# Attention outputs made as features by tokens, row sums taken by the product, top-k rounds spread

## The chip, the cores and the metric

The kernel runs on one core of one Trainium2 chip. Its engines are TensorE (PE, with PEld for the loading of its stationary operand), VectorE (DVE), ScalarE (ACT), GpSimd (POOL) and SyncE (SP), which here only issues DMAs. The metric is the device time of one execution in microseconds (us); the median of the runs shown is compared.

## The reference

One streaming step of a hybrid encoder layer on 512 prompt tokens and 64 tokens of a running stream with 128 cached keys (D = 1024, float32). In the part that the change touches, eight query heads with two key/value heads of 64 features attend to keys that an indexer has chosen:

```python
index_score = jnp.einsum('bqh,bqhl->bql', w_idx * IDX_SCALE, jax.nn.relu(dots))
index_score = jnp.where(admissible[None], index_score, -jnp.inf)
_, sel = lax.top_k(index_score, topk)                  # topk = min(256, keys / 4)
...
logits = jnp.einsum('bqgrd,bqkgd->bqgrk', qg, k_sel) * (hd ** -0.5)
p = jax.nn.softmax(jnp.where(valid, logits, -jnp.inf), axis=-1)
o = jnp.einsum('bqgrk,bqkgd->bqgrd', p, v_sel)         # then o @ w_branch_dsa
```

Around it stand an RMSNorm, one input projection (`x @ w_in`), a gated linear recurrence, a merge with gates, and a convolutional feed-forward part. The outputs are the layer's tokens and the new keys, values and states.

## The kernel before

The order of all work in the first part is written out as a list of slots (`plan_slots`). A slot is one weight block of the projection applied to all tokens, or, for the value weights of the recurrence (`gv`), one weight panel applied to one of five token tiles (tile 0: the 64 sample tokens, tiles 1 to 4: 128 prompt tokens each). The four gv panels have five such slots each, with a short slot `z` for the gate logits after the second. Each engine runs through the same list; beside the slot's own work it does what `plan_aux` has put at that slot. Nothing reorders this at run time: every engine works its instructions in order and waits on semaphores.

Attention is put in as 40 steps `("att", n)`, one a slot, 8 heads for each tile in the order 1, 0, 2, 3, 4. Step n is a pipeline over four heads: PE makes the logits of head n (L2260, L2261) and DVE adds the mask and takes the minimum of the negated values (L1666); ACT exponentiates, with the row sum as accumulator (L1127); PE turns the probabilities of head n-2 (L2269) and ACT copies them to SBUF (L1122, for the sample tile L1119); PE multiplies the turned probabilities of head n-3 with the values (L2283), and DVE divides the 64 columns of the head by the row sum (L1673, L1678) into `otok`, tokens by features. After each eighth head PE turns `otok` into features by tokens (L2291), and ACT copies that to `aqt` (L1137), in which the queries of the same tile stood. Since the turn uses a logits bank, PE waits at steps 12, 20, 28 and 36 for that copy (`o_ready`). Every fourth step also splits four heads of queries for the next tile into a rounded part (ACT L1055, `q_split`) and its remainder (DVE L1593).

The mask of tiles 0, 2, 3, 4 comes from top-k on DVE: a round takes the 8 largest scores (MAX8, L1651) and strikes them out (L1652). Tile 0 has 6 rounds of 192 keys, the others 16 rounds each of 256, 384 and 512 keys. `plan_aux` gives out rounds by a budget: each slot from the first attention step on adds `ATT_ROOM` to it, and a round of w keys takes 2w + 220 from it:

```python
while n < len(rounds) and AT_IDX + rounds[n][0] < s and room > 0:
    put(s, ("topk", rounds[n:n + 1]))
    room -= 2 * width(IDX_TILES[rounds[n][0]]) + 220
    n += 1
```

DVE also does a scan for each `z` slot, one slot later (L1686, L1687, L1689, after a softplus on ACT, L1142 to L1144), and three multiplications two slots after that (L1694 to L1698). The split of a weight panel into rounded part and remainder is ACT's (L960) and, for the panels of this stretch, POOL's (L789); from the `gr` panels on DVE does it (L1531). POOL also stores the new keys and values to HBM before its first split. All products are sums of three (rounded times rounded, and the two cross terms with the remainders), except those in attention and recurrence in plain float32.

Of the kernel before, what the change touches and what calls it, by code (L numbers as in the profile page):

```python
# [178 lines left out]
ATT_ROOM = 1800  # L179
# [121 lines left out]
def layer_kernel(nc, A, O):  # L301
# [6 lines left out]
    with ExitStack() as ctx:  # L308
# [49 lines left out]
        v_low = at("v_low", [P, TILES, 148], F32, o1 + 15872 + 5120)  # L358
        cache = at("cache", [P, 3, P], F32, o1 + 23968)
# [19 lines left out]
        otok = at("otok", [P, QH * HD], F32, o3 + 16128)  # L379
# [70 lines left out]
        probs_turned, pt_ready, pv_done, o_scaled = sem("probs_turned"), sem("pt_ready"), sem("pv_done"), sem("o_scaled")  # L450
        o_turned, o_ready = sem("o_turned"), sem("o_ready")
# [152 lines left out]
        def _(sp):  # L604
# [17 lines left out]
            def saved_load(k):  # L622
                b, j = SAVED_BUFFER[k], SAVED[k]
                if k == 0:
                    sp.wait_ge(o_ready, len(ATT_TILES))
# [20 lines left out]
            for p in range(UP0 + SEVEN0):  # L646
                load(p)
                for what, k in SAVED_MOVES.get(p, ()):
                    if what == "in":
                        saved_load(k)  # L650
                    else:
                        saved_store(k)
                if p == 0:
                    for tt in range(2, TILES):
                        load_x(tt)
                if p == 1:
                    ck, cv = A["cache_k"][0, 0], A["cache_v"][0, 0]
                    sp.dma_start(cache[:, 0, :], ck.rearrange("s g d -> s (g d)")).then_inc(cache_loaded, 16)
                    sp.dma_start(cache[:, 1, :], cv.rearrange("s g d -> s (g d)")).then_inc(cache_loaded, 16)
                    for half in range(2):  # L660
                        sp.dma_start(cache[:, 2, half * 64:half * 64 + 64], A["cache_k_idx"][0, 0]).then_inc(cache_loaded, 16)
                    sp.wait_ge(xlo_ready, 2 * TILES)
                    sp.dma_start(wgu_in[0:RANK, :], A["w_gla_gate_up"][0]).then_inc(wgu_loaded, 16)
# [73 lines left out]
        def _(pool):  # L737
# [29 lines left out]
            pool.wait_ge(coefs_turned, 1)  # L767
            link(nc.gpsimd.memset(bias0[:, :], 0.0))
# [11 lines left out]
            pool.dma_start(O["v_s"][0, 0].rearrange("s g d -> s (g d)"), v_low[0:DEC, 0, 20:148]).then_inc(stored, 16)  # L780

# [11 lines left out]
            for s, slot in enumerate(SLOTS):  # L793
# [7 lines left out]
                for op, n in AUX.get(s, []):  # L801
# [17 lines left out]
                    if op == "gla":  # L819
                        step, tt = GLA_STEPS[n]  # L820
                        if n == 0:
                            pool.wait_ge(o_ready, len(ATT_TILES))
# [121 lines left out]
        def _(act):  # L944
# [61 lines left out]
            for tt in range(TILES):  # L1006
                act.wait_ge(kv_done, tt + 1)
                nc.scalar.activation(k_idx[:, tt, 0:192], ps[:, tt, 0:192], ACT.Copy)
                nc.scalar.activation(k_idx[:, tt, 192:256], ps[:, tt, 128:192], ACT.Copy)
                nc.scalar.activation(v_low[:, tt, :], ps[:, tt, 192:340], ACT.Copy).then_inc(kv_copied, 1)  # L1010
# [46 lines left out]
            def aux(op, n):  # L1057
# [53 lines left out]
                elif op == "att":  # L1111
# [19 lines left out]
                    m = n - 4  # L1131
                    if m >= 0 and m % QH == QH - 1:
                        t = m // QH
                        tt = ATT_TILES[t]
                        act.wait_ge(o_turned, t + 1)
                        k = rows(tt)
                        nc.scalar.activation(aqt[:, :, tok(tt).start:tok(tt).start + k],  # L1137
                                             ps[:, 4 + (n + 1) % 2, :].rearrange("p (b c) -> p b c", b=4)[:, :, 0:k], ACT.Copy).then_inc(o_ready, 1)
# [376 lines left out]
        def _(dve):  # L1515
# [80 lines left out]
            def aux(op, n):  # L1596
# [58 lines left out]
                elif op == "att":  # L1655
# [14 lines left out]
                    if 0 <= m < NATT:  # L1670
                        h = m % QH
# [5 lines left out]
                        g = h // (QH // KVH)  # L1677
                        nc.vector.tensor_scalar(otok[:, HD * h:HD * h + HD], ps[:, 7, HD * g:HD * g + HD],  # L1678
                                                rinv[:, m % 2:m % 2 + 1], None, ALU.mult).then_inc(o_scaled, 1)
# [387 lines left out]
        def _(pe):  # L2067
# [141 lines left out]
            def aux(op, n):  # L2209
# [6 lines left out]
                elif op == "keyt":  # L2216
# [10 lines left out]
                    pe.transpose(ps[:, 7, 0:128], cache[:, 0, :], ident[:, :])  # L2227
                    pe.transpose(ps[:, 7, 128:192], k_idx[0:DEC, 0, 0:128], i64)
                    pe.transpose(ps[:, 7, 192:320], cache[:, 2, :], ident[:, :])
# [15 lines left out]
                elif op == "att":  # L2245
                    if n < NATT:
# [11 lines left out]
                        if n >= 12 and (n - 5) % QH == QH - 1:  # L2258
                            pe.wait_ge(o_ready, (n - 5) // QH + 1)
# [12 lines left out]
                    if 0 <= m < NATT:  # L2272
                        tt = ATT_TILES[m // QH]
                        pe.wait_ge(pt_ready, m + 1)
                        if m >= 1:
                            pe.wait_ge(o_scaled, m)
                        blocks = key_blocks(tt)
                        for i, (c, k) in enumerate(blocks):
                            if tt == 0:
                                val = cache[:, 1, :] if i == 0 else v_low[0:DEC, 0, 20:148]  # L2280
                            else:
                                val = v_low[:, i + 1, 20:148]
# [3 lines left out]
                    m = n - 4  # L2286
                    if m >= 0 and m % QH == QH - 1:

                        pe.wait_ge(o_scaled, m + 1)
                        for b in range(4):  # L2290
                            ins = pe.transpose(ps[:, 4 + (n + 1) % 2, P * b:P * b + P], otok[:, P * b:P * b + P], ident[:, :])  # L2291
                        ins.then_inc(o_turned, 1)
                elif op == "gla":
                    step, tt = GLA_STEPS[n]
                    stream = 0 if tt == 0 else 1
                    if step == "a":
                        if n == 0:
                            pe.wait_ge(sample_values, 5)
                            pe.wait_ge(decay_used, 3 * GH)
                            pe.wait_ge(o_ready, len(ATT_TILES))  # L2300
# [251 lines left out]
```

## Time and profile before

| | us |
|---|---|
| median of 3 runs (973.52 to 974.26) | 973.52 |
| the profiled execution | 974.0 |
| its span, first to last instruction | 972.3 |
| PE busy (98% of the span) | 955.3 |
| DVE busy (64%) | 617.5 |
| ACT busy (49%) | 476.3 |
| POOL busy (19%) | 181.0 |

The granted clock of TensorE is 0.999 of full speed over the span, 2.4 GHz. Attention lies between 86.8 us, the first logits, and 271.6 us, the last copy of the outputs. A row of the timeline or of the chain gives the start and the length in us; in square brackets stands how long the engine was idle before it and who released it. Lengths of PE instructions overlap, so that the spacing of starts, not the length, says what one of them costs.

### The profile page before, as it was taken

Reading aid. Unit: us, or ns where it says so; the run is one execution under the profiler, and the core shown is the slowest. Engines: PE = TensorE matmul, PEld = TensorE weight load, DVE = VectorE, ACT = ScalarE, POOL = GpSimd, SP = SyncE. Lnnn points to the kernel's source line nnn. Section 1 sums busy time; section 2 is a strip of 40 time slices with the busy share of each in tenths; the row PEclk is TensorE's granted clock in tenths of the full one; section 3 lists DMA queues with packets and bytes.
Section 4 is the critical chain, followed back from the end, with each engine's and each line's share of the span. In section 5 each row is a group of like instructions: output and inputs, shape, how many; then the busy total and the mean of one; then the engine's idle time right before and its main releaser. Section 6 shows DMA issues by size and latency. Waiting matters only on the chain.

```text
span 972.3 us, 17124 instructions
## 1 busy us (share of the span) xinstructions
PE 955.3 (98%) x6550; PEld 904.3 (93%) x6550; DVE 617.5 (64%) x997; ACT 476.3 (49%) x800; POOL 181.0 (19%) x301
## 2 busy tenths in 40 slices
PE   8999999999999999999999999999999999999997
PEld 6999998889999999999998899999999999788886
DVE  6278878745344368924455679688888889723214
ACT  6356436777322256421124558566666667522112
POOL 3104423323122111101001146211111112100000
PEclk9999999999999999999999999999999999999999
DMA  6812121112376458766446352244443344412323
GB/s 169 205 45 87 44 88 44 44 44 67 122 235 223 139 209 268 262 242 227 125 135 239 129 174 87 76 121 127 150 123 119 119 128 131 145 36 84 137 70 119
DMA packets 121980, 129.75 MB, mean 133 GB/s; under 512 B 14884, under 2 KB 103828, under 8 KB 119619
## 3 DMA queue, kind: packets, MB, share of 16 engines
q1 hardware_dynamic: 115474, 105.97, 35.0%
q0 software_dynamic: 6448, 22.99, 6.7%
q8 instruction: 39, 0.64, 0.3%
q14 instruction: 19, 0.15, 0.0%
HBM read 105.84 MB, written 23.11 MB: 133 GB/s over the span
## 4 chain that ended last, share of the span: by engine, by line
PE 90%; DVE 4%; ACT 3%; issue 2%; DMA 0%; POOL 0%; DVEq 0%; SPq 0%; ACTq 0%; POOLq 0%
PE ps L2078 11%; PE ps L2080 11%; PE ps L2079 11%; PE ps L2443 7%; PE ps L2445 7%; PE ps L2444 7%; PE ps L2087 7%; PE ps L2089 7%; PE ps L2088 7%; PE ps L2283 2%; PE ps L2097 1%; PE ps L2098 1%; PE ps L2420 1%; PE ps L2419 1%; PE ps L2418 1%
## 5 line engine op out<-in xcount | busy, mean ns | idle before, releaser
L2078 PE MATMUL ps<-xs,whi 128*128 128x288 f32 x608 | 183.4, 302 | 0.0
L2080 PE MATMUL ps<-xs,wlo 128*128 128x288 f32 x608 | 179.1, 295 | 0.0
L2079 PE MATMUL ps<-xs,whi 128*128 128x288 f32 x608 | 179.0, 294 | 0.0
L1531 DVE TENSOR_TENSOR wlo<-raw,whi 128x2048 fp32r<-128x2048 f32 (+2 forms) x36 | 78.9, 2193 | 107.9 <-ACT whi L960 107.9
L960 ACT ACTIVATE whi<-raw 128x2048 fp32r<-128x2048 f32 (+2 forms) x47 | 86.1, 1833 | 99.3 <-PE ps L2089 76.4
L2078 PEld LDWEIGHTS ps<-xs,whi 128*128 128x128 f32 x608 | 114.2, 188 | 0.7
L2079 PEld LDWEIGHTS ps<-xs,whi 128*128 128x128 f32 x608 | 114.2, 188 | 0.4
L2080 PEld LDWEIGHTS ps<-xs,wlo 128*128 128x128 f32 x608 | 114.0, 188 | 0.0
L2087 PE MATMUL ps<-whi,xs 128*128 128x256 f32 (+2 forms) x224 | 72.7, 325 | 0.1
L2089 PE MATMUL ps<-wlo,xs 128*128 128x256 f32 (+2 forms) x224 | 71.2, 318 | 0.0
L2088 PE MATMUL ps<-whi,xs 128*128 128x256 f32 (+2 forms) x224 | 71.2, 318 | 0.0
L789 POOL TENSOR_TENSOR wlo<-raw,whi 128x512 fp32r<-128x512 f32 x36 | 45.8, 1303 | 128.6 <-ACT whi L960 128.6
L2089 PE MATMUL ps<-wlo,us 128*128 128x512 f32 x176 | 69.5, 395 | 0.0
L2087 PE MATMUL ps<-whi,us 128*128 128x512 f32 x176 | 69.5, 395 | 0.0
L2088 PE MATMUL ps<-whi,us 128*128 128x512 f32 x176 | 69.5, 395 | 0.0
L2445 PE MATMUL ps<-ts,wlo 128*128 128x288 f32 x216 | 63.9, 296 | 0.0
L2444 PE MATMUL ps<-ts,whi 128*128 128x288 f32 x216 | 63.7, 295 | 0.0
L2443 PE MATMUL ps<-ts,whi 128*128 128x288 f32 x216 | 63.5, 294 | 0.0
L2087 PEld LDWEIGHTS ps<-whi,xs 128*128 128x128 f32 x224 | 42.5, 190 | 3.2 <-DVE xs L1557 0.4
L2089 PEld LDWEIGHTS ps<-wlo,xs 128*128 128x128 f32 x224 | 42.5, 190 | 2.5
L2088 PEld LDWEIGHTS ps<-whi,xs 128*128 128x128 f32 x224 | 42.5, 190 | 2.4
L1040 ACT ACTIVATE stage<-ps 128x576 f32<-128x576 f32 x24 | 15.6, 652 | 57.6 <-PE ps L2080 57.6
(370 smaller groups left out, 2616.8 us busy)
## 6 DMA issues: line engine op xcount, KB each, us to landing
raw<-in_w_in SPq DMA_DIRECT2D x21, 1024.0 KB, 5.8
raw<-in_w_down SPq DMA_DIRECT2D x10, 1024.0 KB, 5.0
saved<-in_w_up SPq DMA_DIRECT2D x36, 256.0 KB, 4.3
sums_scratch<-saved SPq DMA_DIRECT2D x9, 1024.0 KB, 4.8
raw<-sums_scratch SPq DMA_DIRECT2D x9, 1024.0 KB, 4.8
qraw<-in_w_up SPq DMA_DIRECT2D x27, 256.0 KB, 2.9
raw<-in_w_up SPq DMA_DIRECT2D x13, 512.0 KB, 4.0
raw<-in_w_up SPq DMA_DIRECT2D x26, 256.0 KB, 4.5
```

What stands on the lines that cost most here:

```text
L789: ins = nc.gpsimd.tensor_tensor(wlo[:, p % 2, c], raw[:, p % 2, c], whi[:, p % 2, c].bitcast(F32), ALU.subtract)
L960: nc.scalar.activation(whi[:, p % 2, 0:n], raw[:, p % 2, 0:n], ACT.Copy).then_inc(hi_ready, 1)
L1531: nc.vector.tensor_tensor(wlo[:, p % 2, 0:n], raw[:, p % 2, 0:n], whi[:, p % 2, 0:n].bitcast(F32), ALU.subtract).then_inc(lo_ready, 1)
L2078: pe.matmul(out, wh[:, k, c0:c0 + P], xh[:, k, t], start=(k == 0), stop=False)
L2079: pe.matmul(out, wh[:, k, c0:c0 + P], xl[:, k, t], start=False, stop=False)
L2080: ins = pe.matmul(out, wl[:, k, c0:c0 + P], xh[:, k, t], start=False, stop=(k == kn - 1))
L2087: pe.matmul(out, xh[:, k0 + k, t], wh[:, k, :], start=(first and k == 0), stop=False)
L2088: pe.matmul(out, xl[:, k0 + k, tl or t], wh[:, k, :], start=False, stop=False)
L2089: ins = pe.matmul(out, xh[:, k0 + k, t], wl[:, k, :], start=False, stop=(last and k == kn - 1))
L2443: pe.matmul(out, wh[:, c], xh[:, k, :], start=(opens and k == 0), stop=False, skip_group_check=True)
L2444: pe.matmul(out, wh[:, c], xl[:, k, :], start=False, stop=False, skip_group_check=True)
L2445: ins = pe.matmul(out, wl[:, c], xh[:, k, :], start=False, stop=(k == 3), skip_group_check=True)
```

## The change

The values become the stationary operand of the product and the turned probabilities the moving one, so the product comes out as features by tokens and needs no turn. Beside the 64 value features of a head's group stand 64 columns of ones, so the other 64 rows of the same product hold the row sum, once in each row. DVE takes the reciprocal of those 64 rows (64 x 128) and multiplies the 64 rows of features by it, straight into `aqt`. For the ones, `v_low` becomes 64 columns wider, and POOL moves the values of the second group and sets the ones after the stores; the cached values are loaded in two pieces with room for ones between. `otok`, its turn, the copy by ACT, the accumulator of the exponential and the waits on both go; `o_ready` is now given once a head. `ATT_ROOM` falls from 1800 to 1300.

```diff
-ATT_ROOM = 1800
+ATT_ROOM = 1300
...
# SP: load of the cached values
-sp.dma_start(cache[:, 1, :], cv.rearrange("s g d -> s (g d)")).then_inc(cache_loaded, 16)
+sp.dma_start(cache[:, P:P + 4 * HD].rearrange("p (a b) -> p a b", b=HD)[:, 0:3:2, :], cv).then_inc(cache_loaded, 16)
...
# POOL, behind the stores
+pool.wait_ge(stored, 16 * 6)
+link(nc.gpsimd.tensor_copy(v_low[:, :, 20 + 2 * HD:20 + 3 * HD], v_low[:, :, 20 + HD:20 + 2 * HD]))
+nc.gpsimd.memset(v_low[:, :, 20 + HD:20 + 2 * HD], 1.0).then_inc(values_spread, 1)
...
# ACT, step n
 nc.scalar.activation(lg[:, n % 3, 0:w], lg[:, n % 3, 0:w], ACT.Exp, bias=negmax[:, n % 3:n % 3 + 1],
-                     scale=-1.0, accum_out=rowsum[:, n % 4:n % 4 + 1]).then_inc(probs_ready, 1)
+                     scale=-1.0).then_inc(probs_ready, 1)
...
-        act.wait_ge(o_turned, t + 1)
-        nc.scalar.activation(aqt[:, :, tok(tt).start:tok(tt).start + k],
-                             ps[:, 4 + (n + 1) % 2, :].rearrange("p (b c) -> p b c", b=4)[:, :, 0:k], ACT.Copy).then_inc(o_ready, 1)
...
# DVE, step n, head m = n - 3
-dve.wait_ge(probs_ready, m + 1)
-link(nc.vector.reciprocal(rinv[:, m % 2:m % 2 + 1], rowsum[:, m % 4:m % 4 + 1]))
 dve.wait_ge(pv_done, m + 1)
-if m >= QH and h == 0:
-    dve.wait_ge(o_turned, m // QH)
-nc.vector.tensor_scalar(otok[:, HD * h:HD * h + HD], ps[:, 7, HD * g:HD * g + HD],
-                        rinv[:, m % 2:m % 2 + 1], None, ALU.mult).then_inc(o_scaled, 1)
+link(nc.vector.reciprocal(rec[of_v, 0:k], ps[of_sum, 7, 0:k]))
+nc.vector.tensor_tensor(aqt[half, h // 2, tok(tt).start:tok(tt).start + k], ps[of_v, 7, 0:k], rec[of_v, 0:k],
+                        ALU.mult).then_inc(o_ready, 1)
...
# PE, step n
-if n >= 12 and (n - 5) % QH == QH - 1:
-    pe.wait_ge(o_ready, (n - 5) // QH + 1)
...
-if m >= 1:
-    pe.wait_ge(o_scaled, m)
+if m == 0:
+    pe.wait_ge(values_spread, 1)
+    pe.wait_ge(pads_zero, 3)
+else:
+    pe.wait_ge(o_ready, m)
...
-    ins = pe.matmul(ps[:, 7, 0:128], pt[0:k, m % 2, P * i:P * i + P], val,
+    ins = pe.matmul(ps[:, 7, 0:q], val, pt[0:k, m % 2, P * i:P * i + q],
                     start=(i == 0), stop=(i == len(blocks) - 1))
...
-    pe.wait_ge(o_scaled, m + 1)
-    for b in range(4):
-        ins = pe.transpose(ps[:, 4 + (n + 1) % 2, P * b:P * b + P], otok[:, P * b:P * b + P], ident[:, :])
-    ins.then_inc(o_turned, 1)
```

How instructions stand on two engines, first on DVE at attention steps 26 and 27 (third gv panel, tile 3 with 384 keys), before. `lg` are the masked logits, `score_92` the mask of 384 keys in this list, and the two ISA rows are the masking and its minimum:

```order
L1666 ISA lg,small<-ps,score_92 128x384
L1666 ISA small 128x1
L1673 RECIPROCAL small<-small 128x1
L1678 TENSOR_SCALAR otok<-ps,small 128x64
L1666 ISA lg,small<-ps,score_92 128x384
...
L1593 TENSOR_TENSOR q_split<-aqt,q_split 64x512
L1686 SCALAR_TENSOR_TENSOR tmp<-tmp 128x576
```

The same place after the change, where `score_91` is the mask of 384 keys and `score_92` the scores of 512 keys:

```order
L1662 ISA lg,small<-ps,score_91 128x384
L1662 ISA small 128x1
L1672 RECIPROCAL rec<-ps 64x128
L1673 TENSOR_TENSOR aqt<-ps,rec 64x128
L1647 MAX small<-score_92 128x8
L1648 MATCH_REPLACE score_92<-small,score_92 128x512
L1647 MAX small<-score_92 128x8
L1648 MATCH_REPLACE score_92<-small,score_92 128x512
L1662 ISA lg,small<-ps,score_91 128x384
...
L1589 TENSOR_TENSOR q_split<-aqt,q_split 64x512
L1681 SCALAR_TENSOR_TENSOR tmp<-tmp 128x576
```

Between the two maskings stand now two rounds of top-k of 512 keys, which stood some ten steps earlier before, and the reciprocal has grown from one column to 64 x 128.

On PE at step 19 (end of the first gv panel), where the outputs of the sample tile are turned, before:

```order
L2260 MATMUL ps<-k_hi,q_split 128x256
L2261 MATMUL ps<-k_lo,q_split 128x256
L2269 MATMUL ps<-ident,lg 128x128 x2
L2283 MATMUL ps<-v_low,pt 128x128 x2
L2291 MATMUL ps<-ident,otok 128x128 x4
L2097 MATMUL ps<-whi,xs 128x256
```

The same place after the change:

```order
L2253 MATMUL ps<-k_hi,q_split 128x256
L2254 MATMUL ps<-k_lo,q_split 128x256
L2262 MATMUL ps<-ident,lg 128x128 x2
L2280 MATMUL ps<-pt,v_low 128x128 x2
L2092 MATMUL ps<-whi,xs 128x256
```

The four turns of `otok` are gone, the product has as many instructions as before, with its operands exchanged, and PE goes on to the weights of the next panel.

## Rows read from the trace of the kernel before

**Rows 1.** The page: busy time by engine, and the chain's shares.
```profile
PE 955.3 (98%) x6550; PEld 904.3 (93%) x6550; DVE 617.5 (64%) x997; ACT 476.3 (49%) x800; POOL 181.0 (19%) x301
...
PE 90%; DVE 4%; ACT 3%; issue 2%; DMA 0%; POOL 0%; DVEq 0%; SPq 0%; ACTq 0%; POOLq 0%
```

**Rows 2.** Waits of PE, 80 to 290 us: total, times, longest.
```profile
PE ps L2260 <- ACT aqt L1137: 4.1, 2, 2.3
PE ps L2269 <- ACT pt L1122: 1.4, 2, 0.8
PE ps L2283 <- DVE otok L1678: 1.0, 2, 0.6
```

**Rows 3.** Timeline of PE, steps 20 and 28: idle before, releaser.
```profile
165.97 0.35 PE L2260 MATMUL ps<-k_hi,q_split 128*128 128x256 f32 x1 [1.76 <-ACT aqt L1137]
...
202.85 0.41 PE L2260 MATMUL ps<-k_hi,q_split 128*128 128x384 f32 x1 [2.31 <-ACT aqt L1137]
```

**Rows 4.** Windows: stretch, length, busy PE, PEld, DVE, ACT, POOL, clock, DMA.
```profile
143.80:164.20 20.40, 20.40 (x160) 19.12 (x158) 17.95 (x42) 14.96 (x31) 7.42 (x6) 1.00 0.17 53
164.20:186.80 22.60, 19.05 (x156) 18.45 (x155) 19.85 (x49) 15.28 (x30) 7.58 (x6) 1.00 0.15 47
186.80:210.40 23.60, 20.70 (x171) 20.09 (x170) 11.38 (x31) 18.34 (x36) 6.15 (x6) 1.00 0.15 46
210.40:232.60 22.20, 22.20 (x181) 21.66 (x180) 12.29 (x28) 16.84 (x30) 7.43 (x6) 1.00 0.16 48
```

**Rows 5.** The chain near the last attention steps: start, length.
```profile
267.10 0.89 PE ps L2283 x8
...
271.15 0.44 PE ps L2291 x4
```

**Rows 6.** Timeline of PE in the recurrence: 64 moving columns.
```profile
291.38 0.39 PE L2312 MATMUL ps<-qk,k_cross 128*128 128x64 f32 x2
291.60 0.39 PE L2311 MATMUL ps<-qk 128*128 128x64 f32 x2
```

**Rows 7.** Lines of DVE by form: busy us, mean ns, idle before.
```profile
L1722 DVE RECIPROCAL tmp<-tmp 128x576 f32<-128x576 f32 x4 | 15.0, 3754 | 5.6 <-ACT tmp L1177 5.4
...
L1678 DVE TENSOR_SCALAR otok<-ps,small 128x64 f32<-128x64 f32 x40 | 11.4, 284 | 12.0 <-PE ps L2283 8.1 <-PE ps L2291 3.0
...
L1673 DVE RECIPROCAL small<-small 128x1 f32<-128x1 f32 x40 | 6.3, 158 | 0.0
...
L1932 DVE TENSOR_TENSOR hb<-ps,p 128x64 f32<-128x64 f32 x18 | 3.9, 219 | 0.0
...
L2008 DVE TENSOR_TENSOR us<-u_all,us 128x128 fp32r<-128x128 f32 x1 | 0.3, 283 | 0.0
```

**Rows 8.** Timeline of DVE: rounds of top-k that follow each other.
```profile
117.34 0.55 DVE L1651 MAX8 small<-score 128x8 f32<-128x384 f32 x1
...
118.58 0.56 DVE L1651 MAX8 small<-score 128x8 f32<-128x384 f32 x1
...
142.16 0.68 DVE L1651 MAX8 small<-score 128x8 f32<-128x512 f32 x1
...
143.66 0.69 DVE L1651 MAX8 small<-score 128x8 f32<-128x512 f32 x1
```

**Rows 9.** Waits of DVE, 143.8 to 210.4 us: total, times, longest.
```profile
DVE q_split L1593 <- ACT q_split L1055: 6.7, 4, 4.2
DVE lg L1666 <- PE ps L2261: 6.4, 3, 3.1
DVE tmp L1686 <- ACT tmp L1144: 1.2, 2, 0.9
```

**Rows 10.** Timeline of DVE: the query split of step 27.
```profile
202.26 0.69 DVE L1593 TENSOR_TENSOR q_split<-aqt,q_split 64x512 fp32r<-64x512 f32 x1 [4.16 <-ACT q_split L1055]
```

**Rows 11.** Timeline of POOL: the last store and what follows.
```profile
42.17 0.53 POOL L780 DMA_DIRECT2D out_v_s<-v_low  x1
75.22 5.08 POOL L789 TENSOR_TENSOR wlo<-raw,whi 128x512 fp32r<-128x512 f32 x4 [32.51 <-ACT whi L960]
```

More of the change, by code:

```diff
@@ L378, in layer_kernel @@
         pt = at("pt", [P, 2, 512], F32, o3 + 12032)
-        otok = at("otok", [P, QH * HD], F32, o3 + 16128)
+        cache = at("cache", [P, 3 * P + HD], F32, o3 + 16128)
+        rec = at("rec", [P, P], F32, o3 + 17920)
         gain_row = at("gain_row", [P, D], F32, o3 + 5888)
@@ L657, in _ @@
                     ck, cv = A["cache_k"][0, 0], A["cache_v"][0, 0]
-                    sp.dma_start(cache[:, 0, :], ck.rearrange("s g d -> s (g d)")).then_inc(cache_loaded, 16)
-                    sp.dma_start(cache[:, 1, :], cv.rearrange("s g d -> s (g d)")).then_inc(cache_loaded, 16)
+                    sp.dma_start(cache[:, 0:P], ck.rearrange("s g d -> s (g d)")).then_inc(cache_loaded, 16)
+                    sp.dma_start(cache[:, P:P + 4 * HD].rearrange("p (a b) -> p a b", b=HD)[:, 0:3:2, :], cv).then_inc(cache_loaded, 16)
                     for half in range(2):
-                        sp.dma_start(cache[:, 2, half * 64:half * 64 + 64], A["cache_k_idx"][0, 0]).then_inc(cache_loaded, 16)
+                        sp.dma_start(cache[:, 2 * P + HD + half * 64:3 * P + half * 64], A["cache_k_idx"][0, 0]).then_inc(cache_loaded, 16)
                     sp.wait_ge(xlo_ready, 2 * TILES)
@@ L1009, in _ @@
                 nc.scalar.activation(k_idx[:, tt, 192:256], ps[:, tt, 128:192], ACT.Copy)
-                nc.scalar.activation(v_low[:, tt, :], ps[:, tt, 192:340], ACT.Copy).then_inc(kv_copied, 1)
+                nc.scalar.activation(v_low[:, tt, 0:148], ps[:, tt, 192:340], ACT.Copy).then_inc(kv_copied, 1)
             def copy_unit(slot):
@@ L1670, in aux @@
                     if 0 <= m < NATT:
-                        h = m % QH
-                        dve.wait_ge(probs_ready, m + 1)
-                        link(nc.vector.reciprocal(rinv[:, m % 2:m % 2 + 1], rowsum[:, m % 4:m % 4 + 1]))
+                        tt, h = ATT_TILES[m // QH], m % QH
+                        g = h // (QH // KVH)
+                        k, half = rows(tt), slice(64 * (h % 2), 64 * (h % 2) + 64)
+                        of_v, of_sum = slice(HD * g, HD * g + HD), slice(HD - HD * g, 2 * HD - HD * g)
                         dve.wait_ge(pv_done, m + 1)
-                        if m >= QH and h == 0:
-                            dve.wait_ge(o_turned, m // QH)
-                        g = h // (QH // KVH)
-                        nc.vector.tensor_scalar(otok[:, HD * h:HD * h + HD], ps[:, 7, HD * g:HD * g + HD],
-                                                rinv[:, m % 2:m % 2 + 1], None, ALU.mult).then_inc(o_scaled, 1)
+                        link(nc.vector.reciprocal(rec[of_v, 0:k], ps[of_sum, 7, 0:k]))
+                        nc.vector.tensor_tensor(aqt[half, h // 2, tok(tt).start:tok(tt).start + k], ps[of_v, 7, 0:k], rec[of_v, 0:k],
+                                                ALU.mult).then_inc(o_ready, 1)
                     if n % 4 == 3 and n + 5 < NATT:
@@ L2274, in aux @@
                         pe.wait_ge(pt_ready, m + 1)
-                        if m >= 1:
-                            pe.wait_ge(o_scaled, m)
+                        if m == 0:
[3 more added lines that the diff above has]
+                            pe.wait_ge(o_ready, m)
                         blocks = key_blocks(tt)
+                        q, g = rows(tt), m % QH // (QH // KVH)
                         for i, (c, k) in enumerate(blocks):
                             if tt == 0:
-                                val = cache[:, 1, :] if i == 0 else v_low[0:DEC, 0, 20:148]
+                                val = cache[:, P + HD * g:2 * P + HD * g] if i == 0 else v_low[0:DEC, 0, 20 + HD * g:148 + HD * g]
                             else:
-                                val = v_low[:, i + 1, 20:148]
-                            ins = pe.matmul(ps[:, 7, 0:128], pt[0:k, m % 2, P * i:P * i + P], val,
+                                val = v_low[:, i + 1, 20 + HD * g:148 + HD * g]
+                            ins = pe.matmul(ps[:, 7, 0:q], val, pt[0:k, m % 2, P * i:P * i + q],
                                             start=(i == 0), stop=(i == len(blocks) - 1))
                         ins.then_inc(pv_done, 1)
-                    m = n - 4
-                    if m >= 0 and m % QH == QH - 1:
-                        pe.wait_ge(o_scaled, m + 1)
-                        for b in range(4):
-                            ins = pe.transpose(ps[:, 4 + (n + 1) % 2, P * b:P * b + P], otok[:, P * b:P * b + P], ident[:, :])
-                        ins.then_inc(o_turned, 1)
                 elif op == "gla":
```

23 lines of the change are left out of this document (9 added, 14 removed).

## The prediction

> **What bounds the kernel now.** I read the busy shares and the chain of waits first: TensorE (PE) is busy in 98% of the span and makes up 90% of the chain that ended last [rows 1]. So PE work that goes, or a PE wait that goes, is worth its full length, and work on another engine costs nothing until PE waits for it. Then I read who makes PE wait during the attention stage (80 to 290 us) [rows 2]: 4.1 us for the ScalarE (ACT) copy of the turned outputs, 1.4 us for the ACT copy of the turned probabilities, 1.0 us for the scaling on VectorE (DVE), 6.5 us in all. The two waits of the first kind, 1.76 and 2.31 us, are single places [rows 3]. Last I cut the stretch in which they lie into the four panels of value weights (gv 0 to 3, attention steps 15-19, 20-24, 25-29, 30-34) and read the busy time of each engine in each [rows 4]. PE works 20.40, 19.05, 20.70 and 22.20 us in stretches of 20.4, 22.6, 23.6 and 22.2 us, so all 6.45 us of idle time lie in panels two and three. DVE is busy 17.95, 19.85, 11.38 and 12.29 us: nearly as long as PE in the first two panels, with half its time free in the last two. DVE is the engine behind the stalls, and it is also where the change puts its work.
>
> **The change part by part.**
>
> *Turns that go.* Five times PE turns four blocks of the outputs. In the chain one such group of four takes 0.44 us [rows 5]. 5 x 0.44 = 2.2 us of pure PE time go. The ACT copies and the accumulator reads that go are no gain by themselves: ACT waits for others in this stage.
>
> *The product of probabilities and values.* Stationary and moving operand change places; blocks and passes stay. A product of four blocks takes 0.89 us before [rows 5], and for 128 queries all sizes are the same. For the sample tile the moving side shrinks from 128 to 64 columns in 16 products. The nearest row is in the recurrence stage: a two-pass product with 64 moving columns starts 0.22 us after the one before it [rows 6], and a block of the attention product with 128 columns takes 0.89 / 4 = 0.22 us. I take no gain; the far bound, half of 16 x 0.22 us, is 1.8 us.
>
> *Row sums in the product, division by a tensor.* This is the dear part. Before, each of 40 head products costs DVE a reciprocal of one column, 0.158 us, and a scaling of 64 columns, 0.284 us [rows 7], together 0.44. After, it is a reciprocal of 64 x 128 and a tensor_tensor of 64 x 128 (64 x 64 for the 8 sample products). No such reciprocal is in the trace; the bounds are the one of 576 elements, 3.754 us, and the one of 1 element, 0.158 us [rows 7]. The slope is (3.754 - 0.158) / 575 = 6.25 ns an element, so 128 elements cost 0.158 + 127 x 0.00625 = 0.95 us and 64 cost 0.55 us. The multiplication lies at 0.28 us (128 elements) and 0.22 us (64 elements) [rows 7]. New pair: 1.23 and 0.77 us, that is +0.79 and +0.33 us a product; over all, 32 x 0.79 + 8 x 0.33 = 27.9 us more on DVE. If the reciprocal went at the pace of the tensor_tensor of 128 elements, 0.283 us, the pair would cost 0.57 and the surplus be 0.13 us: that end is kept for a rival. I take the slope, because it comes from the same operation.
>
> The Trainium skill (page "VectorE: DVE Perf Modes", section on the TRN2 errata) gives VectorE one price for every operation that reads PSUM, 120 cycles plus one an element at 0.96 GHz, about 0.26 us here. By that the pair would cost 0.54 us, the surplus be 0.10 us, and the sum come out as in the cheap rival below. The same page says that Reciprocal is an iterative divide with a repeat count, and the trace sides with that: 3.754 us for 576 elements.
>
> *Top-k spread.* ATT_ROOM falls from 1800 to 1300, so the rounds of the largest tile (512 keys, 16 rounds), which stood in panels one and two, move later. From the order of the instructions, rounds of 512 in panels one to four: before 7, 4, 0, 0 (five more earlier), after 4, 5, 5, 2, and two rounds of 384 slip into panel one. A round is MAX8 and MATCH_REPLACE8; two rounds start 1.50 us apart at 512 and 1.24 us at 384 [rows 8].
>
> *DVE by panel.* (The one closing operation of a tile moves with its rounds and is left out.) Panel one: rounds -3 x 1.50 + 2 x 1.24 = -2.0; products 4 x 0.33 + 0.79 = +2.1; sum +0.1. Panel two: one round more, +1.5; five products, +3.95; sum +5.45. Panel three: five rounds, +7.5, and +3.95; sum +11.45. Panel four: two rounds, +3.0, and +3.95; sum +6.95. DVE's work becomes 18.1, 25.3, 22.8 and 19.2 us beside 20.4, 19.05, 20.7 and 22.2 us of PE work. In panels two and three it is DVE that has more to do.
>
> *What PE then waits for.* Over the first three panels DVE has 49.2 + 17.0 = 66.2 us. On top come its waits for ACT in the same stretch, 6.7 us for the query split and 1.2 us for the gate chain [rows 9]; these are in program order and not filled by other work. The longest, 4.2 us before the split of step 27, ends at 202.26 us [rows 10]: two rounds (3.0) and two dearer products (1.6) now fall into the time from step 26 to that split, but ACT's chain starts only when DVE has done step 26, so I let it shrink by 1.1 us only. 66.2 + 6.8 = 73.0 us. PE has 60.15 us less two groups of turns, 59.3. The surplus is 13.7 us. DVE may end the third panel farther behind PE than it began the first, but a product is waited for one step later, and a step is 4 us (20.4 / 5): with some lag at the start already, I allow 3 us. So PE idles 10.7 to 13.7 us; I take 12.0. Panel four, 19.2 us and the gate chain's wait against 22.2, about breaks even, and outside the four panels DVE has room: 12.0 is all.
>
> *The two waits that go* are inside this account: without the wait for the turned copy at step 20 PE meets, right behind it, the scaling of step 16; without the one at step 28 it meets the exponential of step 26 and, a step later, the product behind the DVE scan. What was late next before is later still now.
>
> *Edits at no cost.* POOL now waits for its six stores before it spreads the values, with its weight splits queued behind. The last store is issued at 42.2 us, and the next POOL work starts at 75.2 us after 32.5 us of idle [rows 11]. If that cover were gone, the price would be two POOL operations of 128 x 320, under the 1.3 us that each of a weight split's four operations of 128 x 512 takes (5.08 / 4), so under 2.6 us. The strided load of the cached values, twice as many pieces of half the size, is issued on SP's queue at the program's start and read first in the attention stage. That PE needs the spread values at step 3 costs nothing by the same gap on POOL.
>
> **Sum**, against the profiled execution (974.0 us, span 972.3): -2.2 (turns) + 12.0 - 6.45 (idle after less idle before) = +3.35, 977.35 us. The median of the runs shown, 973.52, is 0.5 us under that execution, so I predict 976.9 us. What this kernel's measurement can tell from no change is about 0.2%, 1.9 us: faster is below 971.6, slower above 975.5.
>
> **Rivals.**
> *A: DVE's free time absorbs it.* Within the first three panels DVE waited 6.4 us for logits of PE [rows 9], free time, and the spread evens out the peaks that stall PE now. Then idle time only grows to about 8 us: 974.0 - 2.2 + 1.5 - 0.5 = 972.9 us, no difference. Against it: the free time lies in panel three, and the rounds moved there (7.5 us) fill it before the dearer products come.
> *B: the reciprocal is cheap, and the kernel faster.* At 0.283 us the products add 4 x 0.1 + 11 x 0.13 = 1.8 us in three panels instead of 10.0, the surplus falls from 13.7 to 5.5, less 0 to 3 carried, so 4.0 us of idle: 974.0 - 2.2 - 2.4 - 0.5 = 968.9 us. It decides from a pair of about 0.6 us. Only the row of 576 elements speaks against it, but it is the same operation. The rule of the skill's page above would end here.
> *C: DVE never catches up.* Nothing is carried (13.7), and two further peaks of the size of the first stall now (1.76) come in panel four and behind it, where the gate scan and the weight splits share DVE with the dearer products: idle 17.2 us, 974.0 - 2.2 + 10.8 - 0.5 = 982.1 us. For it: the last round of top-k now ends one step before its scores are used.
>
> **How the numbers follow.** Forecast 0.50 (975 to 979.5), A 0.20, B 0.13, C 0.17. Faster is B, 0.13. Within 0.2% is A and the lower edge of the forecast, 0.25. Slower is the rest, 0.62. The range reaches down to A with most of the sample products' gain and up to C: 971.5 to 982.0, which leaves out B and the end of C.
>
> **What would show it.** The reciprocal in the profile after: 0.9 to 1.0 us for 64 x 128 proves the price, under 0.4 proves B. PE's idle time between steps 15 and 30 should be 10 to 14 us, released by DVE's multiplication into the features or by ACT's exponential, which itself waits for DVE; no turn and no copy behind it is left. DVE should be busy in over nine tenths of panels two and three. I am wrong if PE idles less than 8 us there, or if it waits on something outside the attention stage.

## The result and the profile after

The changed kernel takes 980.53 us (median of 4 runs, 979.72 to 981.05), the kernel before 973.72 us: ratio 1.0067, interval [1.0055, 1.0079], slower by 6.8 us. Slower was forecast, by 3.4 us; 980.5 lies inside the range. The profiled execution took 980.58 us with a span of 978.8 us, 6.5 us over the span before.

The page of the changed kernel, busy time and the chain's shares, beside [rows 1]:
```profile
PE 956.4 (98%) x6530; PEld 905.3 (92%) x6530; DVE 651.5 (67%) x997; ACT 469.5 (48%) x755; POOL 181.2 (19%) x304
...
PE 86%; DVE 7%; ACT 3%; issue 3%; DMA 0%; POOL 0%; DVEq 0%; SPq 0%; ACTq 0%; POOLq 0%
```
PE's share of the chain fell by 4 points and DVE's rose by 3: more of the path now runs through DVE. Who makes PE wait, 80 to 300 us of the changed kernel (total, times, longest), beside [rows 2]:
```profile
PE ps L2280 <- DVE aqt L1673: 10.5, 8, 3.2
PE ps L2262 <- ACT pt L1126: 1.3, 2, 0.7
PE ps L2262 <- ACT pt L1124: 0.2, 1, 0.2
```
The waits for the turned copy are gone, as they must be. In their place the product of a step waits eight times, 10.5 us in all, for the multiplication that empties its bank; the three lines together are 12.0 us, where the three before were 6.5. What that multiplication stands behind is in the lines of DVE by form (busy us, mean ns, idle before), beside [rows 7]:
```profile
L1672 DVE RECIPROCAL rec<-ps 64x128 f32<-64x128 f32 x32 | 30.6, 955 | 5.6 <-PE ps L2280 4.7
...
L1673 DVE TENSOR_TENSOR aqt<-ps,rec 64x128 f32<-64x128 f32 x32 | 9.2, 289 | 1.1
...
L1672 DVE RECIPROCAL rec<-ps 64x64 f32<-64x64 f32 x8 | 4.4, 555 | 1.5 <-PE ps L2280 1.4
...
L1673 DVE TENSOR_TENSOR aqt<-ps,rec 64x64 f32<-64x64 f32 x8 | 1.8, 222 | 0.3
```
The reciprocal has the price that its slope gave: 0.955 and 0.555 us against 0.95 and 0.55. The four gv panels of the changed kernel (steps 15, 20, 25, 30 and 35 begin at 142.9, 163.6, 187.3, 215.6 and 239.9 us), columns as in [rows 4]:
```profile
142.90:163.60 20.70, 19.63 (x156) 18.71 (x155) 17.86 (x40) 14.79 (x29) 7.08 (x6) 1.00 0.17 53
163.60:187.30 23.70, 20.59 (x157) 19.93 (x156) 22.41 (x42) 15.06 (x26) 7.43 (x6) 0.93 0.15 45
187.30:215.60 28.30, 22.30 (x167) 21.25 (x166) 24.15 (x49) 16.31 (x26) 6.15 (x6) 0.94 0.12 38
215.60:239.90 24.30, 22.43 (x180) 21.49 (x179) 22.79 (x38) 16.60 (x25) 7.59 (x6) 1.00 0.15 45
```
Length less PE's busy time is PE's idle time: 1.1, 3.1, 6.0 and 1.9 us, together 12.05. And there is something that the profiled execution of the kernel before does not show in this stage: in panels two and three the granted clock is 0.93 and 0.94. Cut into microseconds around the longest stall of panel two and that of panel three:
```profile
170.00:171.00 1.00, 0.49 (x3) 0.52 (x4) 0.93 (x3) 0.35 (x2) 0.00 (x0) 0.88 0.00 0
171.00:172.00 1.00, 1.00 (x7) 1.00 (x6) 0.93 (x4) 0.00 (x0) 0.00 (x0) 0.50 0.00 0
...
174.00:175.00 1.00, 1.00 (x10) 1.00 (x10) 0.96 (x3) 1.00 (x2) 0.24 (x1) 0.92 0.09 16
...
211.00:212.00 1.00, 0.63 (x4) 0.66 (x5) 0.94 (x3) 0.97 (x4) 0.00 (x0) 0.86 0.00 0
212.00:213.00 1.00, 1.00 (x7) 1.00 (x6) 0.96 (x3) 1.00 (x3) 0.00 (x0) 0.50 0.00 0
```
At 0.50 (1.2 GHz) the clock stays for 3.4 us each time (0.88, three times 0.50, 0.92 in the first); this is called a half-clock stretch below. The timeline of PE shows what went before, and what it costs:
```profile
170.51 0.97 PE L2280 MATMUL ps<-pt,v_low 128*128 128x128 f32 x4 [2.00 <-DVE aqt L1673]
...
171.76 0.41 PE L2082 MATMUL ps<-whi,xs 128*128 128x256 f32 x1
171.97 0.41 PE L2083 MATMUL ps<-whi,xs 128*128 128x256 f32 x1
...
174.26 0.28 PE L2082 MATMUL ps<-whi,xs 128*128 128x256 f32 x1
174.38 0.29 PE L2083 MATMUL ps<-whi,xs 128*128 128x256 f32 x1
...
211.37 1.31 PE L2280 MATMUL ps<-pt,v_low 128*128 128x128 f32 x6 [3.19 <-DVE aqt L1673]
```
PE had stood still for 2.00 and for 3.19 us. Behind that, weight products start 0.21 us apart instead of 0.12, so a stretch of 3.4 us loses 3.4 x (1 - 0.12 / 0.21) = 1.46 us, the two 2.9 us. First account: idle +5.6, half clock +2.9, turns -2.2 = +6.3 of the 6.5 us of span. Whether the clock is a cause or only the form that a wait takes, the account does not say.

### The profile page after: what moved, and what is told of

It reads as the page before. It is cut to its first block, busy times and chain, and to the rows that moved or that the text cites. A ratio compares the mean times of both kernels' runs of the same rounds, so it can differ in the third digit from the quotient of the medians.

```text
span 978.8 us, 17005 instructions
## 1 busy us (share of the span) xinstructions
PE 956.4 (98%) x6530; PEld 905.3 (92%) x6530; DVE 651.5 (67%) x997; ACT 469.5 (48%) x755; POOL 181.2 (19%) x304
## 4 chain that ended last, share of the span: by engine, by line
PE 86%; DVE 7%; ACT 3%; issue 3%; DMA 0%; POOL 0%; DVEq 0%; SPq 0%; ACTq 0%; POOLq 0%
PE ps L2073 11%; PE ps L2075 11%; PE ps L2074 11%; PE ps L2433 7%; PE ps L2435 7%; PE ps L2434 7%; PE ps L2082 6%; PE ps L2084 6%; PE ps L2083 6%; PE ps L2092 1%; PE ps L2093 1%; PE ps L2410 1%; PE ps L2409 1%; PE ps L2408 1%; PE ps L2280 1%
```

## The experiments

The first theory: DVE has too much to do beside the panels; the reciprocal's price is the cost, the spread moves it, the two falls of the clock add 3 us. Rivals: the spread alone costs; each product is delayed by its own longer way through DVE; the clock fell for another reason. A median below stands beside 973.7 to 974.4 us for the kernel before, measured beside it; ratios are to that.

**The price of the division: a copy in its place.**
```
-  reciprocal(rec[of_v, 0:k], ps[of_sum, 7, 0:k])
+  tensor_copy(rec[of_v, 0:k], ps[of_sum, 7, 0:k])
```


> The changed kernel with the reciprocal replaced by a copy of the same 64 x 128 sums (this leaves out the division: the output is multiplied by the sum). Everything else, the product, the spread and the waits, stays. Theory: the copy takes 0.25 to 0.3 us, DVE has 0.67 us less a product, PE's idle time falls to 4 to 6 us, both half-clock stretches go, 969 to 971 us, faster than the kernel before. Rival 1 (the spread is what costs): idle time stays above 9 us, 976 us or more. Rival 3 (the clock fell for another reason than the long stalls): the stretches at half clock are still there, about 3 us on top.

975.41 us, ratio 1.0016 [1.0007, 1.0025]: 5.1 us under the changed kernel, but not the 969 to 971 expected; PE's idle time is 7.75 us (220 less 212.25), not 4 to 6. The copy takes 0.289 us (64 x 128), so 0.67 us a product is worth 5.1 us in all. What stayed, in PE's timeline of this kernel (idle before, releaser):
```profile
169.85 0.68 PE L2280 MATMUL ps<-pt,v_low 128*128 128x128 f32 x4 [1.99 <-DVE aqt L1673]
...
208.72 1.62 PE L2280 MATMUL ps<-pt,v_low 128*128 128x128 f32 x6 [2.54 <-DVE aqt L1673]
```
The two long stalls stand, and a half-clock stretch follows each. The theory misses something that is not the reciprocal's price alone.

**DVE's time without the longer way**: before, with a reciprocal that nobody reads.
```
     tensor_scalar(otok[...], ps[...], rinv[...], None, ALU.mult)
+    reciprocal(spare[0:64, 0:k], ident[0:64, 0:k])
```


> The kernel before with a spare reciprocal (64 x 128, for the sample 64 x 64) on DVE behind each scaling, into a tile that nothing reads: DVE's time for the division without its place in the chain from product to next product, with the old order of the top-k rounds and the old turns. Theory (DVE's sum of work in panels one to three is what delays PE): 0.95 us a product, 5 us in each panel, PE's idle time in the attention stage rises from 6.5 to 11 to 14 us, 978 to 981 us. Rival 2 (it is the longer way from a product to the next one through DVE that PE waits for): 974 to 975.5 us.

979.49 us, ratio 1.0060 [1.0046, 1.0074], +5.7 us: as the theory has it, and the rival, that only the longer way costs, falls. The stalls take another form than expected. PE's waits in this kernel, 80 to 300 us:
```profile
PE ps L2263 <- ACT aqt L1138: 5.3, 3, 2.3
PE ps L2272 <- ACT pt L1123: 2.0, 2, 1.8
PE ps L2286 <- DVE otok L1679: 0.7, 2, 0.5
```
Nearly all of it is put down to ACT, although only DVE got more work: ACT's exponential and copies stand behind DVE's masking, for which ACT waits 40.5 us between 80 and 300 us (19.9 before). PE is idle for 8.65 us there (220 less 211.35 busy), 2.2 more than before, not the expected 5 to 8 more. One half-clock stretch (185 to 189 us) adds 1.5, and 0.5 us lie ahead of the stage (first logits at 87.35 us, 86.84 before); 0.7 us of the 4.9 us of span I can't place.

**No spread.**
```
-ATT_ROOM = 1300
+ATT_ROOM = 1800
```


> The changed kernel with ATT_ROOM back at 1800: dear division, no spread of the top-k rounds. Theory (DVE has too much to do beside the panels: the reciprocal's price is the cost, the spread only moves it, and the clock falls add to it): DVE then has about 20, 24, 15 and 16 us of work in the four panels, so only panel two is over PE's 19 us, and the idle time moves forward and shrinks from 12 to 8 to 11 us; 975 to 979 us, nearer the lower end if no stall reaches 2 us and the clock stays up. Rival 1 (the spread is what costs, the division alone is absorbed): 971 to 973 us. Rival 2 (each product is delayed by its own chain product, reciprocal, multiplication, whatever the order): 980 to 981 us, stalls as many as with the spread.

978.74 us, ratio 1.0059 [1.0045, 1.0073]: inside the theory's 975 to 979, idle 12.6 us (220 less 207.44) rather than 8 to 11, no half-clock stretch in the profiled execution. The division without the spread costs 5.0 us, the turns' gain already taken off. The five runs lie apart: three at 978.28 to 978.74 us with a mean granted clock of 0.999, two at 980.65 and 980.76 with 0.995, the mean that the changed kernel has with its two half-clock stretches. In this kernel the lower clock goes with 2.2 us more.

**The spread alone**, in the kernel before.
```
-ATT_ROOM = 1800
+ATT_ROOM = 1300
```

> The kernel before with ATT_ROOM 1300 instead of 1800: the spread alone, with the cheap scaling. Theory: the rounds move into panels three and four, where DVE had 9 us and 10 us beside PE's work; idle time of PE stays at 6 to 9 us, the clock stays up, 973 to 976 us. Rival 1 (the spread is what costs): idle of 10 us or more, 978 us or more. A third outcome, that the spread by itself evens DVE out as it is said to: idle of 3 to 5 us, 970 to 972 us.

976.83 us, ratio 1.0030 [1.0019, 1.0041]: +3.1 us, over the theory's 976 and under the rival's 978. Idle time is 7.24 us (6.45 before), but it has gathered in one place. DVE's timeline in this kernel, with ACT's exponential of step 26:
```profile
191.67 0.69 DVE L1651 MAX8 small<-score 128x8 f32<-128x512 f32 x1
...
193.78 0.62 ACT L1127 ACTIVATE lg<-lg,small 128x384 f32<-128x384 f32 x1 [0.81 <-DVE small L1666]
...
197.76 0.28 DVE L1678 TENSOR_SCALAR otok<-ps,small 128x64 f32<-128x64 f32 x1
203.30 0.69 DVE L1593 TENSOR_TENSOR q_split<-aqt,q_split 64x512 fp32r<-64x512 f32 x1 [5.26 <-ACT q_split L1055]
```
ACT's same exponential in the kernel before:
```profile
192.74 0.61 ACT L1127 ACTIVATE lg<-lg,small 128x384 f32<-128x384 f32 x1
```
And PE's timeline with the spread, at step 28:
```profile
203.90 0.47 PE L2260 MATMUL ps<-k_hi,q_split 128*128 128x384 f32 x1 [3.48 <-ACT aqt L1137]
```
A round that moved here (191.67 us) stands ahead of the masking of step 26, and ACT's exponential waits for that masking. It starts 1.04 us later than before, and with it all that ACT does next in order: a weight split, the logarithm of the gate chain between two table loads, the high half of the queries and the copy for which PE waits. So PE's stall grows by 1.17 us (3.48 against 2.31), and DVE waits 5.26 us for the high half of the queries, with its next work queued behind. [Rows 10] shows the same wait before, 4.16 us. A half-clock stretch follows the stall of 3.48 us: 0.8 + 1.5 are the 2.3 us of the span.

**The clock**: work for PE in the two long stalls of the changed kernel, ahead of the product's wait.
```
+  if n in (21, 29):
+      pe.wait_ge(masked, n)
+      for _ in range(5 if n == 21 else 6):
+          pe.matmul(ps[:, 4 + (n + 1) % 2, 0:P], ident[:, :], ident[:, :], start=True, stop=True)
```


> The changed kernel with five and six idle products of the identity on PE ahead of the wait for the scaling in steps 21 and 29, behind a wait for the masking of the same step (which DVE ends about 1.3 us earlier than that scaling): the stalls of 2.00 and 3.19 us are cut to about 0.6 and 1.7 us, each followed by work. Theory on the clock (the granted clock fell because PE had stood idle for those 2.00 and 3.19 us): no half-clock stretch behind them, 3.0 us less, 977 to 978.5 us. If one of the two pieces left is still enough for a fall: 979 us. Rival 3 (the fall has another reason): both stretches are still there, 980 to 981.5 us.

979.85 us, ratio 1.0061 [1.0047, 1.0074]: in the profiled execution (980.29 us) the clock stays up, but in the median only 0.7 us come back, not 2 to 3.5. Nor is it the clock that gives these 0.7 us: the three runs with a mean clock of 0.999 took 979.85 to 980.33 us, the two with 0.997 were the quickest (979.53 and 979.57). Windows of this kernel over both places:
```profile
169.00:174.00 5.00, 4.47 (x37) 4.45 (x38) 4.77 (x13) 2.56 (x5) 0.00 (x0) 1.00 0.01 3
208.00:213.00 5.00, 3.11 (x27) 2.90 (x26) 4.83 (x9) 2.72 (x6) 0.00 (x0) 1.00 0.16 58
```
Stalls of 0.69 and 1.89 us, each with work behind it, bring no fall here. So both stretches hang on the two long stalls; that a long stall always brings one does not follow, since the kernel without the spread shows stalls of 2.00 and 2.65 us without. Where the 3 us went is in PE's timeline:
```profile
179.49 0.41 PE L2262 MATMUL ps<-ident,lg 128*128 128x128 f32 x2 [0.91 <-ACT pt L1126]
...
185.15 0.68 PE L2284 MATMUL ps<-pt,v_low 128*128 128x128 f32 x4 [1.36 <-DVE aqt L1673]
...
220.40 0.91 PE L2284 MATMUL ps<-pt,v_low 128*128 128x128 f32 x6 [0.85 <-DVE aqt L1673]
```
The changed kernel has no such wait at the first and third of these places and 0.87 us at the second; later it waits 0.69 us where this one waits 0.97 (230.2 us): 0.91 + 0.49 + 0.85 + 0.28 = 2.5 us of new waits. What PE loses at half clock is, in this kernel, time in which DVE catches up. My theory's third part falls for this kernel: the clock did not add 3 us, it took the place of 2.5 us of waiting.

**The wait in DVE's order**: the low half of the queries' split one attention step later, in the changed kernel and in the kernel before.
```
-  if n % 4 == 3 and n + 5 < NATT:
-      query_lo(n // QH + 1, n % QH // 4)
+  if n % 4 == 0 and 4 <= n < NATT - 4:
+      query_lo((n - 1) // QH + 1, (n - 1) % QH // 4)
```


> The changed kernel with DVE's low half of the queries' split moved one attention step later (the numbers are wanted four steps later still). DVE now waits 3.12 us in front of it, to 205.78 us, for ScalarE behind two table loads, with the scan, the next masking and the next scaling queued behind it. Theory (DVE has too much to do in panels two and three, and a wait in its program order counts as work): the stall of 3.19 us at step 29 falls under 1 us and the second half-clock stretch goes with it, the one at step 21 stays; 976.5 to 978.5 us. If DVE waits for the scan's input instead (ScalarE's logarithm): 979.5 to 980.5 us, the same stall.

976.89 us, ratio 1.0031 [1.0018, 1.0043]: 3.6 us under the changed kernel. The wait in the changed kernel, on DVE:
```profile
205.78 0.69 DVE L1589 TENSOR_TENSOR q_split<-aqt,q_split 64x512 fp32r<-64x512 f32 x1 [3.12 <-ACT q_split L1059]
```
What is left with the move, on PE:
```profile
193.16 1.16 PE L2280 MATMUL ps<-pt,v_low 128*128 128x128 f32 x4 [2.04 <-DVE aqt L1673]
...
207.88 0.91 PE L2280 MATMUL ps<-pt,v_low 128*128 128x128 f32 x6 [0.25 <-DVE aqt L1673]
```
At step 29 a stall of 0.25 us is left of 3.19. The edit moves all eight low halves, but in the changed kernel DVE waits in front of one only. So a wait of 3.12 us in DVE's program order (for ACT, with the scan and the masking behind it) was worth about half of the whole loss, and no row of busy time shows it. Not as expected, the stall at step 21 did not stay: it fell from 2.00 to 1.17 us, with no half-clock stretch. Another stall, of 2.04 us at 193 us (1.32 in the changed kernel) with such a stretch behind it, has come in.

> The kernel before with the same move of DVE's low half by one step. DVE's waits for the split (7.5 us in five) shrink to under 2 us, but the two stalls behind ScalarE's copy of the turned outputs have their own cause and stay: 972.5 to 974 us, no difference. If the stall of 2.31 us comes by way of DVE's late masking, which the exponential ahead of that copy waits for: 971 to 972 us.

973.62 us, ratio 0.9994 [0.9985, 1.0003], no difference: the copy of the turned outputs still comes late. Its 11 times lie in two groups, 971.37 to 971.84 us (3) with a mean granted clock of 0.999 and 973.57 to 974.09 us (8) with 0.997; the profiled one, of the upper group, has a half-clock stretch behind the stall of 2.31 us. The kernel before, measured beside it, takes 973.6 us in the median of its runs at 0.999. So the move alone gains some 2 us where the clock stays up, and in most executions the fall takes them back.

**ScalarE's copy first**, in the kernel before: the copy of the turned outputs ahead of the exponential of its step.
```
+  m = n - 4
+  if m >= 0 and m % QH == QH - 1:
...
+      nc.scalar.activation(aqt[...], ps[...], ACT.Copy).then_inc(o_ready, 1)
   if n < NATT:
...
       nc.scalar.activation(lg[...], lg[...], ACT.Exp, ...).then_inc(probs_ready, 1)
...
-  m = n - 4
-  if m >= 0 and m % QH == QH - 1:
...
-      nc.scalar.activation(aqt[...], ps[...], ACT.Copy).then_inc(o_ready, 1)
```

> The kernel before with ScalarE's copy of the turned outputs moved ahead of the exponential of the same step: behind the table load and the exponential it came 2.4 us after the copy of the probabilities in step 28. If these two single places are worth their length: both stalls of 1.76 and 2.31 us fall under 0.6 us, 971 to 972.5 us. If what stands behind them on DVE (its wait for the split of the queries to 202.26 us) is late next: the idle time moves to the product or to the masking's followers, 973 to 974 us, no difference.

974.13 us, ratio 1.0005 [0.9996, 1.0014], no difference. Both old stalls are gone, and others are late next, as the second branch has it. PE's timeline of this kernel:
```profile
170.26 0.68 PE L2283 MATMUL ps<-v_low,pt 128*128 128x128 f32 x4 [1.86 <-DVE otok L1678]
...
206.86 1.09 PE L2283 MATMUL ps<-v_low,pt 128*128 128x128 f32 x6 [1.98 <-DVE otok L1678]
```

**Both moves, in the kernel before:** the last two diffs together.

> The kernel before with both moves: ScalarE's copy of the turned outputs ahead of the exponential, and DVE's low half of the queries one step later. Each alone left a stall of about 2 us, by another cause: the copy behind the table load in the one, DVE's scaling behind its wait for the split in the other. Theory (the two causes cover each other): with both gone no stall reaches 1.5 us, the clock stays up, idle time in the attention stage 3 to 5 us, 970 to 972 us, faster than the kernel before by 2 to 3 us. Rival: a third cause stands behind the two (the probabilities' copy, or the scaling again): idle time of 6 us, 973 to 974.5 us.

969.33 us, ratio 0.9954 [0.9941, 0.9968]: faster than both kernels, by 4.4 and by 11.2 us, and under the expected 970 to 972, although one stall of 1.63 us is left, over the 1.5 expected. PE's waits in this kernel, 80 to 300 us:
```profile
PE ps L2269 <- ACT pt L1122: 2.2, 2, 1.6
PE ps L2283 <- DVE otok L1678: 0.9, 2, 0.6
```
Two moves whose medians show nothing apart are worth 4.4 us together. PE's idle time between 80 and 300 us is 6.45 us before, 5.6 with the low half later, 5.9 with the copy first and 3.1 with both: each alone mostly uncovered the other's wait, and in the profiled execution of either alone a half-clock stretch stands behind a stall that was left.

**Both moves and the spread**, in the kernel before: the last one, and
```
-ATT_ROOM = 1800
+ATT_ROOM = 1300
```

> The kernel before with both moves and the spread (ATT_ROOM 1300), against the same with 1800 (969.3 us). The spread alone made the kernel before 3.1 us slower, with a stall of 3.48 us in step 28, where DVE waited 5.3 us for the split. Theory (the spread costs nothing by itself; it had put rounds next to that wait, which stopped DVE and made the stall long enough for a clock fall): with the wait gone no stall reaches 1.8 us, 968.5 to 970.5 us. Rival (the rounds moved to panels three and four delay the masking and the scaling there whatever the waits): stalls of 2 us or more in panel three, 971.5 to 973 us.

969.19 us, ratio 0.9948 [0.9934, 0.9962]. No stall over 0.91 us is left:
```profile
PE ps L2269 <- ACT pt L1122: 1.8, 3, 0.8
PE ps L2260 <- ACT aqt L1130: 0.9, 1, 0.9
PE ps L2283 <- DVE otok L1678: 0.4, 1, 0.4
```
With both moves the spread costs nothing. So its 3.1 us were made by what it ran into, ACT's late chain and the stall at its end. Which of the two moves takes them away in this kernel, no run separates; the copy first is the one that lies on PE's way to that stall.

**The changed kernel without the spread and with the later low half:** the diff of the low half, and
```
-ATT_ROOM = 1300
+ATT_ROOM = 1800
```

> The changed kernel with ATT_ROOM 1800 and DVE's low half one step later. Theory: DVE's sum of work is the same, so only the wait of 3.5 us for the split in panel three goes; the stall of 2.65 us at step 29 falls under 1 us, those of panel two stay; 976 to 977.5 us, no better than with the spread and the same move (976.9). If the spread costs by itself, as it does in the kernel before (3.1 us there): 974 us.

977.73 us, ratio 1.0038 [1.0024, 1.0052], just over the expected range. With the spread and the same move it was 976.89: no loss by the spread here either. Without the move the changed kernel is 1.8 us slower with the spread (980.53 against 978.74), but the two runs without it at a mean clock of 0.995 take as long (980.65 and 980.76).

**The same with the copy in place of the reciprocal:** this last, and
```
-  reciprocal(rec[of_v, 0:k], ps[of_sum, 7, 0:k])
+  tensor_copy(rec[of_v, 0:k], ps[of_sum, 7, 0:k])
```

> The same kernel as the one before it in this list, but with a copy in place of the reciprocal (this leaves out the division: the output is multiplied by the sum): what the form of the change would give if the division cost no more than a copy. Theory: DVE's work per panel is about that of the kernel before, the turns' 2.2 us and the wait for the split go: 969.5 to 971.5 us. Rival (the new form costs something beside the reciprocal, as the 975.4 us of the copy with the spread may mean): 973 us or more.

968.67 us, ratio 0.9946 [0.9933, 0.9960], somewhat under the expected 969.5 to 971.5. The rival falls: the new form has no large price beside the reciprocal. The reciprocal costs 977.73 - 968.67 = 9.1 us here over a copy, and even without it the new form would be only 0.7 us from the kernel before with both moves (969.33), inside both intervals: of the turns' 2.2 us little is left to see.

## Why the prediction was right in its sign and short by half

**The bound, the turns, the division.** PE's waits decide and DVE makes them: right. The dearer pair came as worked out (0.955 + 0.289 against 1.23; 0.555 + 0.222 against 0.77), over all 46.0 us in place of 17.7 (40 x 0.442), +28.3 against 27.9. Rival B, the cheap reciprocal, falls, and with it the rule of the Trainium skill (page "VectorE: DVE Perf Modes", section on the TRN2 errata) that would have given an estimate of about 0.26 us: 0.955 us is measured, and the measurement decides. That the spare reciprocal on DVE alone made the old kernel 5.7 us slower shows that it is DVE's time that costs.

**What PE then waits for.** For the first three panels I put DVE at 66.2 us of work and 6.8 us of waits, 73.0 us; they last 20.7 + 23.7 + 28.3 = 72.7 us. Work was less than thought (64.4 us) and so were the waits (3.1 us for the split, 1.7 for the gate chain, 0.7 others); the other 2.8 us are short gaps between instructions, which I had not counted. So the sum stood partly by luck. Of the signs that I named, DVE's busy share of over nine tenths held in panel two (22.41 of 23.7 us) and not in panel three (24.15 of 28.3). PE's own work in these panels is 62.5 us, less 2.9 for the half clock 59.6, against 59.3. So PE lost 13.1 us in three panels, where 13.7 was the upper end and 12.0 was taken: the allowance of up to 3 us for DVE's lag was too generous by 1.1 us.

**"Outside the four panels DVE has room: 12.0 is all", and panel four "about breaks even".** This is the step that failed. DVE worked 22.8 us in panel four, not 19.2, beside 22.4 of PE, and PE lost 1.9 us there. Two lines of DVE there account for most of these 3.6 us:
```profile
216.07 0.76 DVE L1689 TENSOR_TENSOR krem<-qk,tmp 128x576 f32<-128x576 f32 x1
...
225.64 1.33 DVE L1650 TENSOR_SCALAR score<-score 128x512 f32<-128x512 f32 x1
```
The first begins the gate chain's three multiplications (to 218.08 us), of which 1.4 us lay in panel three before: the lag that I allowed DVE at the end of panel three was work for panel four. The second is the closing operation of the largest tile, left out of my sums as moving with its rounds; it came into panel four with the last round, at 1.33 us. Rival C had named such peaks (two of 1.76 us). 1.1 + 1.9 = 3.0 us, nearly all of the 3.2 us between 977.35 and 980.58.

**The idle time of 12.0 us that I forecast is the 12.05 us that the trace shows, and for a wrong reason.** PE lost 15.0 us: 12.05 standing still and 2.9 at half clock. No term of the sum was for the clock. Without the fills the reader would put the miss down to that; they show that in this kernel the loss is set by DVE and the clock only decides how much of it is idle. That is no rule: with the spread alone the sum of span comes out with the half clock's 1.5 us in full, and in the kernel without the spread the runs at the lower mean clock are 2.2 us longer.

**The top-k spread** I took as DVE work moved between panels. As such it costs nothing (969.19 against 969.33). It cost 3.1 us in the kernel before by where it put a round: ahead of a masking for which ACT waits before its gate chain, the split and the copy. I had counted DVE's waits for the split as 6.7 us and shrunk the longest by 1.1 (it did shrink by 1.04, to 3.12), without asking what was queued behind it or ahead of it.

**The two waits that go**: "what was late next before is later still now" held; the copy moved first in the old kernel shows the same, no gain in the median from two stalls of 4.1 us.

## What to carry to other kernels

When a stall of the bounding engine goes, look at once for the wait behind it, and take both away before judging either: here two edits without a measurable gain apart gave 4.4 us together. Before making a helper engine's work cheaper, look in its program order for waits with urgent work behind them: moving one wait by a step gave 3.6 us, while the reciprocal's price over a copy was 5.1 us with the same waits in place (9.1 us with the split later and without the spread). And a term of lost clock counts in full only where the bounding engine would not have had to wait anyway; in this case it gave anything from 0.3 us, in the profiled execution with the fills, to about 2 us.

## What the chip showed that I had not expected

PE's granted clock fell to 0.50 for about 3.4 us behind single stalls of 1.98 (the copy first), 1.99, 2.00, 2.04, 2.54, 3.19 and 3.48 us, and twice behind two smaller ones in a row (1.76 and 0.26 with the spare reciprocal; 1.45 and 1.18 in the changed kernel without the spread and with the later low half). It did not behind others of 1.86 (the copy first), 2.00 and 2.65 (without the spread), 2.31 and 2.34 us (the spare reciprocal). Behind the same stall of 2.31 us it stayed up in the kernel before and fell in the one with the low half later. The length of the stall alone does not decide it; what else does, no run here settles. The two groups of times of that kernel, 2 us apart, come with mean clocks of 0.999 and 0.997, and the kernel without the spread has two such groups (0.999 and 0.995): in one and the same kernel the clock falls in some executions and not in others. Only one execution of each was profiled, so which stall the fall follows in the others is not shown.
